# A two-layer decoder step on one core: the opening of layer 0 laid by contraction tile inside the projection, activations loaded first

## The chip, the cores and the metric

One core of a Trainium2 chip runs the whole program in one launch. The metric is device time in microseconds (us) of that core, and lower is better. The kernel before has been run three times: 2797.97, 2799.43 and 2807.59 us, median 2799.43 us.

## What is computed

Two decoder layers are applied to 1024 prompt tokens and 32 sample tokens (8 sequences of 4), 1056 in all, each 1024 wide. Only the head of layer 0 matters here:

```
mod = silu(c) @ w_ada[l] + b_ada[l]
sh1, sc1, g1, sh2, sc2, g2 = split(mod, 6)
h = rmsnorm(x, g_norm1[l]) * (1 + sc1) + sh1
p = h @ w_in[l] + b_in[l]
```

There are nine conditions: one for all prompt tokens, and one for each of the 8 samples. So sh1 and sc1 are 1024 x 9 numbers each, and every one of them is a sum over 1024 rows of w_ada. The columns of p go to three groups of heads; then follow an output projection, a second normalisation, an MLP and two residuals. The forgetting attention of the samples also needs the running sums of cached log-forget values, which are fetched by page ("past sums") for both layers at once.

## The kernel before, in words

**Layout.** Activations lie feature-major: 128 partitions, 8 contraction tiles (KT) of 1056 tokens. A full-precision product is made of three: each operand is split into a high and a low part, and high x high, high x low and low x high are added in PSUM. `part_product` (L303 to L309) issues these three matmuls for one contraction tile and one third (352) of the tokens. A panel is 128 output columns: 8 tiles x 3 thirds x 3 products = 72 matmuls. Its weights come by DMA into `raw`, GpSimd copies the high part (`split_high`, L291), VectorE subtracts it (`split_low`, L297).

**The opening (L384 to L557)** is a block of its own, which ends with all engines meeting. SyncE loads the conditions, then the first 8 blocks of w_ada (1 MB each, 256 columns each) through four buffers, with the constants and the two halves of x between them. In the order of `TURN` the four blocks of sc1 come first, then the four of sh1. For every block i, TensorE does `rows` (L469; the 9 conditions against 256 columns, 8 matmuls on column strips of the array), ScalarE copies the result (L455), TensorE does `fold` (L480; adds the four strips and turns them to columns), and VectorE adds the bias into `mod` (L532). Beside this, ScalarE squares x and VectorE adds the squares (L177, L186), TensorE sums them over partitions (L203), ScalarE takes the root (L231), VectorE the reciprocal (L546), and TensorE spreads it to all partitions (L215). Two tiles are scaled by it already here (L254). The past sums are made here too: a gather by GpSimd (L441), a scan by VectorE (L526), an offset by TensorE (L489), an addition (L538) and eight stores (L396).

**The projection (from L700)** is the next block. Its ScalarE shifts and scales each tile with `mod` (L241), then rounds it to the high part (L243); its VectorE scales the rows and makes the low part (`scale_rows`, L256; `lower_half`, L245). The 256 sample values of each partition go apart (`sample_columns`, L260). TensorE does panels 0 and 1 together in `panel_pair` (L340), tile by tile; then L1014; then panels 2 to 20 (L853), one third after another, with pieces of other work between the thirds. SyncE first stores the whole of x to `x_spill` (L741), since later panels overwrite it, and stage `out_and_mlp` loads it again.

**What sets the order.** Each engine has one queue in program order, and waits on semaphores. VectorE's list for layer 0 of the projection is: low part of panel 1's weights, the rows, the bias, `split_low(2)`, `split_low(3)`, `log_forget`, `split_low(4)`, `maxima`, `split_low(5)`, `averages(0)`, `split_low(6)`, and so on. Panel n can't start before `split_low(n)`.

Of the kernel before, what the change touches and what calls it, by code (L numbers as in the profile page):

```python
# [59 lines left out]
def trunk(nc, xT, cT, consts, suffix, params, g_final, w_first, first_params, w_ada, next_params, w_in, w_out, w_ff, state, hist, kv, lfT, pages,  # L60
# [47 lines left out]
    wada = [tile(f"wada{s}", [P, KT, 256], aL0 + 8192 * s) for s in range(4)]  # L108
# [48 lines left out]
    few = tile("few", [P, KT, NS], F0 + 20 * ROW + 2048)  # L157
    plain = [tile(f"plain{s}", [P, SEQ], F0 + (8 + s) * ROW) for s in range(4)]
# [30 lines left out]
    i_in, i_x, i_con, i_cond, i_sig, i_cs = (sem(f"start_{n}") for n in ("loaded", "rows_in", "constants", "conditions", "sigmoid", "silu"))  # L189
    i_seg, i_scan, i_off, i_sum, i_out, i_suf = (sem(f"start_{n}") for n in ("segments", "scanned", "offsets", "sums", "sums_out", "suffix"))  # L190
    i_g = [sem(f"start_gathered{l}") for l in range(LAYERS)]
    a_loaded = [sem(f"start_ada{s}") for s in range(4)]
    a_done, a_taken, a_folded, a_moved, a_padded = (sem(f"start_ada_{n}") for n in ("done", "taken", "folded", "moved", "padded"))
    pages_n = lfT.shape[0] // LAYERS
    HP = HC * PG
    Glf = [tile(f"Glf{l}", [P, HC, PG], aH0 + 4 * HP * l) for l in range(LAYERS)]
    seg = tile("seg", [P, HC, PG], aH0 + 4 * HP * LAYERS)
    suf = tile("suf", [P, P], aH0 + 4 * HP * (LAYERS + 1))
    none = tile("none", [(8 - HC) * NB, PAST // 4], aH0 + 4 * HP * (LAYERS + 1) + 512)
    first_rows = [tile(f"first_rows{s}", [P, 256], T0 + 1024 * s) for s in range(2)]  # L200
    cw = tile("cw", [P, KT, 32], T0 + 2048)
    sig = tile("sig", [P, KT * 9], T0 + 3072)
# [33 lines left out]
    def modulate(act, N, sc, sh, tiles=range(KT)):  # L236

        for k in tiles:
            t = plain[k % 4]
            act.wait_ge(N["scaled"], k + 1)  # L240
            nc.scalar.activation(t[:], t[:], ACT.Identity, scale=mod[:, sc + k, 0:1], bias=mod[:, sh + k, 0:1]).then_inc(N["modded"], 1)  # L241
            act.wait_ge(N["modded"], k + 1)
            nc.scalar.activation(aH[:, k, 0:SEQ], t[:], ACT.Copy).then_inc(N["high"], 1)  # L243

    def lower_half(dve, N, k):  # L245

        dve.wait_ge(N["high"], k + 1)
        nc.vector.tensor_tensor(aL[:, k, 0:SEQ], plain[k % 4][:], aH[:, k, 0:SEQ].bitcast(F32), ALU.subtract).then_inc(N["low"], 1)

    def scale_tile(dve, N, k):  # L250

        if k >= 4:
            dve.wait_ge(N["low"], k - 3)
        nc.vector.tensor_tensor(two(plain[k % 4][:]), two(x[:, k, 0:SEQ]), PS[:, 6:8, :], ALU.mult).then_inc(N["scaled"], 1)  # L254

    def scale_rows(dve, N, sc, sh):  # L256

        link = chain_on(dve, N["chain"])

        def sample_columns():  # L260
            f4 = few[:].rearrange("p k (b t) -> p k b t", b=NB)
            token = lambda first: mod[:, first:first + KT, 1:9].rearrange("p k (b o) -> p k b o", o=1).to_broadcast([P, KT, NB, NT])
            rs_ = PS[:, 5, 480:512].rearrange("p (o n) -> p o n", o=1).to_broadcast([P, KT, NS])
            link(nc.vector.tensor_tensor(few[:], x[:, :, SEQ:TOK], rs_, ALU.mult))
            link(nc.vector.tensor_tensor(f4, f4, token(sc), ALU.mult))
            link(nc.vector.tensor_tensor(f4, f4, token(sh), ALU.add))
            link(nc.vector.tensor_copy(aH[:, :, SEQ:TOK], few[:]))
            nc.vector.tensor_tensor(aL[:, :, SEQ:TOK], few[:], aH[:, :, SEQ:TOK].bitcast(F32), ALU.subtract).then_inc(N["few"], 1)
        scale_tile(dve, N, SCALED_EARLY)
        sample_columns()  # L270
        lower_half(dve, N, 1)
        for k in range(SCALED_EARLY + 1, KT):
            scale_tile(dve, N, k)
            lower_half(dve, N, k - 1)
        lower_half(dve, N, KT - 1)
# [64 lines left out]
    def panel_pair(pe, s, N, high, low):  # L340

        for k in range(KT):
            pe.wait_ge(N["low"], k + 1)
            if k == 0:
                for p in range(2):
                    pe.wait_ge(s["split"], p + 1)
                    for part in range(NCH - 1):
                        part_product(p, part, k, high, low)
                pe.wait_ge(N["few"], 1)
            for p in range(2):  # L350
                for part in range(NCH - 1 if k == 0 else 0, NCH):
                    last = part_product(p, part, k, high, low)
                if k == KT - 1:
                    last.then_inc(s["done"], NCH)

# [18 lines left out]
    BLOCKS = 2 * KT // 2  # L374
    first = len(sems)
    i_norm.update(norm("norm1", ROOTS + ("scaled", "modded", "high", "low")))
    SCALED_EARLY = 2
    i_par = sem("in_parameters")
    i_w, first_load, first_high, first_low = stream("in", lambda n: w_in[n:n + 1])
    TURN = [BLOCKS // 2 + i for i in range(BLOCKS // 2)] + list(range(BLOCKS // 2))  # L380
    SUMMED_AT, SPREAD_AT = 5, 6
    squared_after = {1: (0, 1, 2, 3), 2: (4, 5), 3: (6, 7)}
    OFFSETS_AT = {2: 0, 3: 1}
    with nc.Block() as block:  # L384
        @block.sync
        def _(sp):
            def ada(i):
                if i >= 4:
                    sp.wait_ge(a_done, i - 3)
                    sp.wait_ge(a_loaded[(i - 2) % 4], 16 * ((i - 2) // 4 + 1))  # L390
                sp.dma_start(wada[i % 4][:], w_first[TURN[i]]).then_inc(a_loaded[i % 4], 16)

            def sums_out(l):
# [3 lines left out]
            sp.dma_start(cs[:], cT).then_inc(i_cond, 16)  # L397
            with nc.allow_non_contiguous_dma(reason="one page a partition"):
                sp.dma_start(pcol[:], pages.rearrange("a n -> n a")).then_inc(i_cond, 16)
            ada(0)  # L400
            sp.dma_start(con[:], consts).then_inc(i_con, 16)
            sp.dma_start(nxt[:], first_params).then_inc(i_con, 16)
            ada(1)
            sp.dma_start(suf[:], suffix).then_inc(i_suf, 16)
            def rows_in(half):
                k = slice(KT // 2 * half, KT // 2 * (half + 1))
                sp.dma_start(x[:, k, :], xT[:, k, :]).then_inc(i_x, 16)
            sp.wait_ge(a_loaded[0], 16)
            rows_in(0)
            sp.wait_ge(a_loaded[1], 16)  # L410
            ada(2)
            sp.wait_ge(i_x, 16)
            rows_in(1)
            sp.wait_ge(i_seg, 3)
            for l in range(LAYERS):
                for q in range(4):
                    sp.dma_start(past_sums[l, 8 * q + HC:8 * q + 8].rearrange("r b n -> (r b) n"), none[:]).then_inc(i_out, 16)
            sp.wait_ge(a_loaded[2], 16)
            ada(3)
            sp.wait_ge(i_x, 32)  # L420
            ada(4)
            ada(5)
            first_load(sp, 0)
            ada(6)
            first_load(sp, 1)
            ada(7)
            sp.dma_start(par[:], params[0]).then_inc(i_par, 16)
            for l in range(LAYERS):
                sums_out(l)
            sp.dma_start(gfin[:], g_final).then_inc(i_in, 16)  # L430
            sp.dma_start(ptab[:], pages).then_inc(i_in, 16)
            sp.wait_ge(i_in, 32)
            sp.wait_ge(i_out, 16 * 8 * LAYERS)

        @block.gpsimd
        def _(pool):
            nc.gpsimd.memset(seg[:], 1.0).then_inc(i_seg, 1)
            nc.gpsimd.memset(none[:], 0.0).then_inc(i_seg, 1)
# [5 lines left out]
            for n in range(2):  # L444
                first_high(pool, n)

        @block.scalar
        def _(act):
            act.wait_ge(i_cond, 32)
            nc.scalar.activation(sig[:], cs[:].rearrange("p a b -> p (a b)"), ACT.Sigmoid).then_inc(i_sig, 1)  # L450
            for i in range(BLOCKS):
                act.wait_ge(a_done, i + 1)
                if i >= 2:
                    act.wait_ge(a_folded, i - 1)
                nc.scalar.activation(first_rows[i % 2][:], PS[:, i % 2, 0:256], ACT.Copy).then_inc(a_taken, 1)  # L455
                if i == SUMMED_AT:
                    root(act, i_norm)
                for j in squared_after.get(i, ()):
                    act.wait_ge(i_x, 16 if j < KT // 2 else 32)
                    square(act, i_norm, j, ss, sq_last)  # L460
# [6 lines left out]
        def _(pe):  # L467
            def rows(i):
                pe.wait_ge(a_loaded[i % 4], 16 * (i // 4) + 16)  # L469
                if i >= 2:  # L470
                    pe.wait_ge(a_taken, i - 1)
# [23 lines left out]
            for i in range(BLOCKS):  # L495
                rows(i)
                if i >= 1:
                    fold(i - 1)
# [2073 lines left out]
```

## Time and profile before

| | |
|---|---|
| runs of the kernel | 2797.97, 2799.43, 2807.59 us; median 2799.43 us |
| span of the profiled execution | 2801.3 us, from first to last instruction; no time outside it is recorded |
| TensorE matmul busy | 2711.2 us (97%) |
| VectorE, ScalarE, GpSimd busy | 1234.9, 644.0, 263.6 us |
| mean granted TensorE clock | 0.987 |
| DMA | 295.37 MB, mean 105 GB/s |

The last instruction's chain is nearly all TensorE. So the time is read by stretches: where TensorE waits, and what releases it.

### The profile page before, as it was taken

The numbers are of one execution on the slowest core, as the hardware profiler recorded it, in microseconds if no ns is written. First come the engines' busy times: TensorE is split into PE (matmuls) and PEld (weight loads), VectorE is DVE, ScalarE is ACT, GpSimd is POOL, SyncE is SP. The second block draws the span as 40 slices with busy tenths as digits, with TensorE's granted clock in tenths as the row PEclk, the third lists the DMA queues.
The fourth block names the chain that finished last, engine by engine and source line by source line (L and its number), as shares of the span: only waits on it lengthen the run. The fifth ranks groups of instructions, "written<-read, shape, count | busy, mean of one in ns | idle before, by whom it ended". The sixth has DMA issues, their size and how long they took to land. (4 is left out here: it accounts for less than half of the span.)

```text
span 2801.3 us, 48407 instructions
## 1 busy us (share of the span) xinstructions
PE 2711.2 (97%) x20524; PEld 2531.6 (90%) x20524; DVE 1234.9 (44%) x2205; ACT 644.0 (23%) x1058; POOL 263.6 (9%) x344
## 2 busy tenths in 40 slices
PE   5999989999999999999999999899999999999998
PEld 4999976699999999999989999666999999999998
DVE  5625535557423423324457354456563243242344
ACT  4334324423101101001132442343221000000012
POOL 1101100020000000001111110001100000000010
PEclk9999999999999999999999999899999999999999
DMA  8440159731222221111134101895212111111111
GB/s 310 151 108 31 67 211 328 265 115 40 82 91 85 82 91 58 56 46 46 61 112 118 51 31 62 296 347 214 75 49 79 46 46 50 42 59 46 46 55 69
DMA packets 106873, 295.37 MB, mean 105 GB/s; under 512 B 19605, under 2 KB 32790, under 8 KB 104610
## 3 DMA queue, kind: packets, MB, share of 16 engines
q1 hardware_dynamic: 106498, 291.49, 30.6%
q8 instruction: 163, 2.67, 0.4%
q0 software_dynamic: 160, 0.79, 0.1%
q14 instruction: 52, 0.43, 0.0%
HBM read 269.61 MB, written 22.63 MB: 104 GB/s over the span
## 5 line engine op out<-in xcount | busy, mean ns | idle before, releaser
L307 PE MATMUL PS<-hH,whi 128*128 128x352 f32 x1632 | 533.9, 327 | 8.2 <-DVE hL L2300 6.6
L307 PE MATMUL PS<-hL,whi 128*128 128x352 f32 x1632 | 524.9, 322 | 0.0
L307 PE MATMUL PS<-hH,wlo 128*128 128x352 f32 x1632 | 524.5, 321 | 0.0
L307 PE MATMUL PS<-aH,whi 128*128 128x352 f32 x1344 | 439.9, 327 | 4.0 <-PEq L384 3.5
L307 PE MATMUL PS<-aL,whi 128*128 128x352 f32 x1344 | 432.8, 322 | 0.0
L307 PE MATMUL PS<-aH,wlo 128*128 128x352 f32 x1344 | 432.3, 322 | 0.0
L295 POOL CAST whi<-raw 128x1024 fp32r<-128x1024 f32 x158 | 167.1, 1058 | 1660.1 <-PE PS L307 1332.7
L307 PEld LDWEIGHTS PS<-hH,whi 128*128 128x128 f32 x1632 | 307.4, 188 | 16.9 <-issue 12.7
L307 PEld LDWEIGHTS PS<-hL,whi 128*128 128x128 f32 x1632 | 308.0, 189 | 0.0
L307 PEld LDWEIGHTS PS<-hH,wlo 128*128 128x128 f32 x1632 | 307.3, 188 | 0.0
L853 PE MATMUL PS<-aH,whi 128*128 128x352 f32 x912 | 304.6, 334 | 1.9 <-ACT F L1053 1.9
L853 PE MATMUL PS<-aH,wlo 128*128 128x352 f32 x912 | 294.9, 323 | 0.0
L853 PE MATMUL PS<-aL,whi 128*128 128x352 f32 x912 | 294.6, 323 | 0.0
L307 PEld LDWEIGHTS PS<-aH,whi 128*128 128x128 f32 x1344 | 253.8, 189 | 9.4 <-issue 4.7
L307 PEld LDWEIGHTS PS<-aL,whi 128*128 128x128 f32 x1344 | 254.3, 189 | 0.0
L307 PEld LDWEIGHTS PS<-aH,wlo 128*128 128x128 f32 x1344 | 253.6, 189 | 0.0
L300 DVE TENSOR_TENSOR wlo<-raw,whi 128x1024 fp32r<-128x1024 f32 x160 | 195.6, 1223 | 130.5 <-POOL whi L295 129.0
L2384 DVE TENSOR_TENSOR aH<-ev 128x1056 fp32r<-128x1056 f32 x64 | 84.2, 1315 | 272.1 <-ACT ev L2269 272.1
L2269 ACT ACTIVATE ev<-PS 128x1056 f32<-128x1056 f32 x64 | 67.5, 1055 | 573.0 <-PE PS L307 573.0
L853 PEld LDWEIGHTS PS<-aH,whi 128*128 128x128 f32 x912 | 172.9, 190 | 8.5 <-issue 4.2
L853 PEld LDWEIGHTS PS<-aL,whi 128*128 128x128 f32 x912 | 173.3, 190 | 0.4
L853 PEld LDWEIGHTS PS<-aH,wlo 128*128 128x128 f32 x912 | 173.0, 190 | 0.0
(369 smaller groups left out, 3633.7 us busy)
## 6 DMA issues: line engine op xcount, KB each, us to landing
KVp<-kv SPq DMA_DIRECT2D x256, 384.0 KB, 7.2
raw<-w_ff SPq DMA_DIRECT2D x128, 512.0 KB, 3.6
raw<-w_in SPq DMA_DIRECT2D x42, 512.0 KB, 3.6
wad_single<-w_ada SPq DMA_DIRECT2D x40, 512.0 KB, 3.6
wad<-w_ada SPq DMA_DIRECT2D x32, 512.0 KB, 5.6
x_spill<-x SPq DMA_DIRECT2D x2, 4224.0 KB, 14.0
wada<-w_first SPq DMA_DIRECT2D x8, 1024.0 KB, 6.8
raw<-w_out SPq DMA_DIRECT2D x16, 512.0 KB, 4.4
```

The source lines that it names most:

```text
L295: nc.gpsimd.tensor_copy(home(n)[0][:], raw[spot(n)][:]).then_inc(s["high"], 1)
L300: nc.vector.tensor_tensor(wl[:], raw[spot(n)][:], wh[:].bitcast(F32), ALU.subtract).then_inc(s["split"], 1)
L307: last = nc.tensor.matmul(PS[:, 3 * p + part, 0:CW], w[:, k, :], a[:, k, part * CW:(part + 1) * CW], start=k == 0 and w is wh and a is hig ...
L853: last = nc.tensor.matmul(PS[:, part, 0:CW], w[:, k, :], a[:, k, part * CW:(part + 1) * CW], start=k == 0 and w is whi[n % 2] and a is aH, ...
L2269: nc.scalar.activation(three(ev[n % 2][:]), banks(n % 2), ACT.Relu).then_inc(s["room"], NCH)
L2384: link(nc.vector.tensor_tensor(aH[:, j, :], t, t, ALU.mult))
```

## The change

- The opening's block is gone; its work is issued at the head of the projection's block in layer 0.
- SyncE loads x first, in four quarters, then the constants, then the 8 blocks of w_ada with at most two on the way, each in a buffer of its own. The host lays w_first out so that block k holds the 128 columns of sh1 and the 128 of sc1 for contraction tile k.
- `modulate` is split differently: VectorE multiplies x by the scale and by the root in one instruction (`scale_tile`), ScalarE adds the shift and rounds (`higher_half`), VectorE adds the shift and subtracts (`lower_half`). There are 3 buffers `plain` in place of 4.
- TensorE goes through the tiles: `rows(k + 2)`, two thirds of panels 0 and 1 for tile k (12 matmuls), `fold(k + 2)`. The last thirds of both panels (48 matmuls) come after all tiles.
- The past sums move behind the opening: GpSimd gathers after `few`; VectorE scans before `split_low(3)` and adds the offsets after `split_low(4)`; TensorE makes the offsets in panel 3; the stores are issued at panel 6.
- Layer 0 no longer stores x to `x_spill`; it is loaded again from the input.

The core of the diff:

```diff
-    wada = [tile(f"wada{s}", [P, KT, 256], aL0 + 8192 * s) for s in range(4)]
+    wada = [tile(f"wada{k}", [P, KT, 256], a) for k, a in enumerate((aL0 + 4 * ROW, aL0 + 6 * ROW, aH0 + 4 * ROW, aH0 + 6 * ROW,
+                                                                     F0 + 15 * ROW, F0 + 17 * ROW, T0 + 2 * ROW, T0))]
...
+    def scale_tile(dve, N, k):
+
+        if k >= len(plain):
+            dve.wait_ge(N["low"], k - len(plain) + 1)
+        nc.vector.scalar_tensor_tensor(two(plain[k % len(plain)][:]), two(x[:, k, 0:SEQ]), mod[:, SC1 + k, 0:1], PS[:, 6:8, :], ALU.mult, ALU.mult)\
+            .then_inc(N["scaled"], 1)
+
+    def higher_half(act, N, k):
+
+        act.wait_ge(N["scaled"], k + 1)
+        nc.scalar.activation(aH[:, k, 0:SEQ], plain[k % len(plain)][:], ACT.Identity, bias=mod[:, SH1 + k, 0:1]).then_inc(N["high"], 1)
...
+        def on_sync(sp):
+            sp.dma_start(cs[:], cT).then_inc(i_cond, 16)
...
+            for q in range(4):
+                k = slice(KT // 4 * q, KT // 4 * (q + 1))
+                sp.dma_start(x[:, k, :], xT[:, k, :]).then_inc(i_x[q], 16)
+            sp.dma_start(con[:], consts).then_inc(i_con, 16)
+            sp.dma_start(nxt[:], first_params).then_inc(i_con, 16)
+            for k in range(KT):
+                if k >= BEFORE:
+                    sp.wait_ge(i_w[k % 2], 16 * (k // 2))
+                sp.dma_start(wada[k][:], w_first[k]).then_inc(i_w[k % 2], 16)
+                if k < 2:
+                    load(sp, k)
...
+        def on_pool(pool):
+            nc.gpsimd.memset(none[:], 0.0).then_inc(i_seg, 1)
+            for n in range(2):
+                split_high(pool, n)
+            pool.wait_ge(N["scaled"], KT)
+            pool.wait_ge(N["few"], 1)
             nc.gpsimd.memset(seg[:], 1.0).then_inc(i_seg, 1)
...
+        def on_tensor(pe):
...
+            def two_thirds(k):
+                pe.wait_ge(N["low"], k + 1)
+                for n in range(2):
+                    if k == 0:
+                        pe.wait_ge(s["split"], n + 1)
+                    for part in range(2):
+                        last = part_product(n, part, k, aH, aL)
+                return last
...
+            sum_squares(pe, N, ss, sq_last[(KT - 1) % 2])
+            rows(0)
+            spread_roots(pe, N)
+            fold(0)
+            rows(1)
+            fold(1)
+            for k in range(KT):
+                if k + 2 < KT:
+                    rows(k + 2)
+                last = two_thirds(k)
+                if k + 2 < KT:
+                    fold(k + 2)
+            last.then_inc(s["done"], 4)
+            pe.wait_ge(N["few"], 1)
+            for n in range(2):
                 for k in range(KT):
...
+                    last = part_product(n, NCH - 1, k, aH, aL)
+                last.then_inc(s["done"], 1)
...
+            def modulation(k):
+                dve.wait_ge(a_folded, k + 1)
...
+                nc.vector.tensor_tensor(mod[:, k:2 * KT:KT, :], folded, b, ALU.add).then_inc(a_moved, 1)
...
+                nc.vector.scalar_tensor_tensor(m, m, 1.0, g, ALU.add, ALU.mult).then_inc(a_gained, 1)
+                dve.wait_ge(a_gained, k + 1)
+            modulation(0)
+            dve.wait_ge(N["spread"], 2)
+            scale_tile(dve, N, 0)
+            split_low(dve, 0)
+            split_low(dve, 1)
+            for k in range(1, KT):
+                modulation(k)
+                scale_tile(dve, N, k)
+                lower_half(dve, N, k - 1)
+            sample_columns(dve, N)
+            lower_half(dve, N, KT - 1)
...
-                sp.dma_start(x_spill, x[:]).then_inc(spilled, 16)
+                    sp.dma_start(x_spill, x[:]).then_inc(spilled, 16)
+                else:
+                    open_sync(sp)
+                    sp.wait_ge(N["few"], 1)
...
+                if not begun:
+                    scans(dve)
                 split_low(dve, 3)
                 log_forget()
                 split_low(dve, 4)
+                if not begun:
+                    add_offsets(dve)
...
-                    sp.dma_start(x[:, :, COLS[ph]], x_spill[:, :, COLS[ph]]).then_inc(reload, 16)
+                    sp.dma_start(x[:, :, COLS[ph]], (x_spill if l else xT)[:, :, COLS[ph]]).then_inc(reload, 16)
```

## Rows read from the trace of the kernel before

**Rows 1.** Windows, panels 0 and 1; columns: stretch, PE, PEld, DVE, ACT, POOL busy, clock, DMA.

```profile
53.10:79.20 26.10, 25.66 (x144) 25.21 (x145) 18.06 (x20) 15.82 (x14) 1.77 (x2) 0.89 0.71 244
```

**Rows 2.** Waits of TensorE, 0 to 330 us; columns: waiter, releaser, sum us, times, longest.

```profile
PE PS L474 <- DMA wada<-w_first: 22.7, 4, 6.8
PE PS L307 <- PEq L384: 3.5, 1, 3.5
PE PS L853 <- ACT F L1053: 1.9, 1, 1.9
```

**Rows 3.** Windows, one stretch of the opening; the last column is GB/s.

```profile
8.00:10.00 2.00, 0.71 (x8) 0.00 (x0) 0.00 (x0) 0.38 (x1) 0.00 (x0) 1.00 1.02 410
```

**Rows 4.** Timeline of TensorE's opening and of L1014; columns: start, us, instructions.

```profile
40.05 1.02 PE L485 MATMUL PS<-con,first_rows 128*128 128x9 f32 x4
41.01 1.08 PE L207 MATMUL PS<-squares,con 128*32 128x256 f32 x8
...
42.95 1.91 PE L474 MATMUL PS<-wada,cw 128*32 128x256 f32 x16
...
45.76 0.70 PE L221 MATMUL PS<-roots,con 32*128 32x256 f32 x4 [0.16 <-DVE roots L546]
...
47.43 1.07 PE L474 MATMUL PS<-wada,cw 128*32 128x256 f32 x16
48.43 1.19 PE L485 MATMUL PS<-con,first_rows 128*128 128x9 f32 x8
...
79.22 0.81 PE L1014 MATMUL PS<-con 128*128 128x384 f32 x2
```

**Rows 5.** Groups of instructions, 0 to 53 us; busy us and mean ns, then idle.

```profile
L186 DVE TENSOR_TENSOR squares<-squares,square_last 128x1056 f32<-128x1056 f32 x6 | 7.5, 1256 | 8.5 <-ACT square_last L177 8.2
L177 ACT ACTIVATE square_last<-x 128x1056 f32<-128x1056 f32 x7 | 7.2, 1074 | 4.7 <-DMA x<-xT 4.3 <-DVE squares L186 0.4
...
L526 DVE TENSOR_TENSOR_SCAN Glf<-seg,Glf 128x768 f32<-128x768 f32 x2 | 3.4, 1746 | 7.5 <-DMA Glf<-lfT,pcol 7.5
...
L546 DVE RECIPROCAL roots<-roots 128x288 f32<-128x288 f32 x1 | 2.0, 1952 | 2.5 <-ACT roots L234 2.5
L538 DVE TENSOR_TENSOR Glf<-Glf,PS 128x768 f32<-128x768 f32 x2 | 1.9, 944 | 0.0
...
L532 DVE TENSOR_TENSOR mod<-PS,nxt 128x18 f32<-128x18 f32 x8 | 1.3, 173 | 7.5 <-PE PS L485 7.5
```

**Rows 6.** Timeline, two neighbouring matmuls of panels 0 and 1.

```profile
60.10 0.32 PE L307 MATMUL PS<-aH,whi 128*128 128x352 f32 x1
60.26 0.32 PE L307 MATMUL PS<-aL,whi 128*128 128x352 f32 x1
```

**Rows 7.** Windows around the start of panel 2; the clock is third from last.

```profile
80.00:82.00 2.00, 0.11 (x2) 0.12 (x2) 1.22 (x1) 1.85 (x2) 1.65 (x2) 1.00 0.66 243
82.00:84.00 2.00, 2.00 (x10) 2.00 (x11) 0.00 (x0) 0.00 (x0) 1.88 (x3) 0.69 0.50 160
84.00:86.00 2.00, 2.00 (x8) 2.00 (x8) 0.00 (x0) 0.99 (x1) 1.94 (x5) 0.50 0.29 117
```

**Rows 8.** Groups of VectorE by form, 1380 to 1480 us: layer 1's norm.

```profile
L633 DVE SCALAR_TENSOR_TENSOR aL<-end_wide,mod,aH 128x704 fp32r<-128x704 f32 x8 | 7.4, 944 | 0.0
L623 DVE SCALAR_TENSOR_TENSOR end_wide<-x,mod,PS 128x704 f32<-128x704 f32 x8 | 7.4, 940 | 0.0
```

**Rows 9.** Timeline of VectorE: first of the five sample instructions, and what follows them.

```profile
55.23 0.41 DVE L264 TENSOR_TENSOR few<-x,PS 128x256 f32<-128x256 f32 x1
...
57.26 1.22 DVE L248 TENSOR_TENSOR aL<-plain,aH 128x1024 fp32r<-128x1024 f32 x1
```

**Rows 10.** Timeline of VectorE and GpSimd in panels 3 to 5 of layer 0.

```profile
101.84 2.27 DVE L1193 TENSOR_TENSOR_SCAN F<-Mrow,LC 6x1024 f32<-6x1024 f32 x1
...
115.32 1.21 DVE L300 TENSOR_TENSOR wlo<-raw,whi 128x1024 fp32r<-128x1024 f32 x1
...
124.33 1.04 POOL L295 CAST whi<-raw 128x1024 fp32r<-128x1024 f32 x1 [12.60 <-PE PS L853]
```

More of the change, by code:

```diff
@@ L156, in trunk @@
     rr = tile("roots", [P, NQ + NS], F0 + 20 * ROW)
-    few = tile("few", [P, KT, NS], F0 + 20 * ROW + 2048)
-    plain = [tile(f"plain{s}", [P, SEQ], F0 + (8 + s) * ROW) for s in range(4)]
+    few = tile("few", [P, KT, NS], F0 + 21 * ROW)
+    plain = [tile(f"plain{s}", [P, SEQ], F0 + (8 + s) * ROW) for s in range(3)]
     def scale_and_gain(first, gain):
@@ L256, in scale_rows @@
-    def scale_rows(dve, N, sc, sh):
-        link = chain_on(dve, N["chain"])
[L260 to L275, printed above, removed]
+        nc.vector.scalar_tensor_tensor(aL[:, k, 0:SEQ], plain[k % len(plain)][:], mod[:, SH1 + k, 0:1], aH[:, k, 0:SEQ].bitcast(F32),
+                                       ALU.add, ALU.subtract).then_inc(N["low"], 1)
@@ L338, in panel_by_tile @@
             after(n)
[L340 to L354, printed above, removed]
     def emptied_panel(act, s, n, func):
@@ L382, in trunk, with opening, sums_out @@
[L382 to L393, printed above, removed]
+    def opening(s, N, load, split_high, split_low, par_loaded):
+        BEFORE = 2
+        def on_sync(sp):
+            sp.dma_start(cs[:], cT).then_inc(i_cond, 16)
+            with nc.allow_non_contiguous_dma(reason="one page a partition"):
+                sp.dma_start(pcol[:], pages.rearrange("a n -> n a")).then_inc(i_cond, 16)
+            for q in range(4):
[9 more added lines that the diff above has]
+                    load(sp, k)
+            sp.dma_start(par[:], params[0]).then_inc(par_loaded, 16)
+            sp.dma_start(suf[:], suffix).then_inc(i_suf, 16)
+            sp.dma_start(gfin[:], g_final).then_inc(i_in, 16)
+            sp.dma_start(ptab[:], pages).then_inc(i_in, 16)
+            sp.wait_ge(i_seg, 1)
+            for l in range(LAYERS):
+                for q in range(4):
+                    sp.dma_start(past_sums[l, 8 * q + HC:8 * q + 8].rearrange("r b n -> (r b) n"), none[:]).then_inc(i_out, 16)
+        def sums_out(sp):
+            for l in range(LAYERS):
@@ L443, in _, with on_scalar @@
                                         element_offset=l * pages_n * HP).then_inc(i_g[l], 16)
[L444 to L448, printed above, removed]
+        def on_scalar(act):
             act.wait_ge(i_cond, 32)
             nc.scalar.activation(sig[:], cs[:].rearrange("p a b -> p (a b)"), ACT.Sigmoid).then_inc(i_sig, 1)
[L451 to L460, printed above, removed]
-            act.wait_ge(a_padded, 3)
-            act.wait_ge(a_moved, BLOCKS // 2 + 1)
-            act.wait_ge(i_out, 16 * 8 * LAYERS)
-            modulate(act, i_norm, SC1, SH1, range(1))
@@ L511, in _, with take @@
-        @block.vector
-        def _(dve):
+            for j in range(KT):
+                act.wait_ge(i_x[j // 2], 16)
+                square(act, i_norm, j, ss, sq_last)
+            root(act, N)
+            def take(k):
+                act.wait_ge(a_done, k + 1)
+                if k >= 2:
+                    act.wait_ge(a_folded, k - 1)
+                nc.scalar.activation(first_rows[k % 2][:], PS[:, 2, 256 * (k % 2):256 * (k % 2) + 256], ACT.Copy).then_inc(a_taken, 1)
+            take(0)
@@ new lines, in on_scalar, with rows, fold @@
+            take(1)
+            for k in range(KT):
+                higher_half(act, N, k)
+                if k + 2 < KT:
+                    take(k + 2)
+        def on_tensor(pe):
+            def rows(k):
+                pe.wait_ge(i_w[k % 2], 16 * (k // 2 + 1))
+                if k >= 1:
+                    pe.wait_ge(a_taken, k)
+                for i in range(KT):
+                    q = i % 4
+                    last = nc.tensor.matmul(PS[32 * q:32 * q + 32, 2, 256 * (k % 2):256 * (k % 2) + 256], cw[:, i, :], wada[k][:, i, :],
+                                            start=i < 4, stop=i >= 4, skip_group_check=True)
+                last.then_inc(a_done, 1)
+            def fold(k):
+                pe.wait_ge(a_taken, k + 1)
+                if k >= 1:
+                    pe.wait_ge(a_moved, k)
+                for n in range(2):
+                    at_ = 32 * (k % 2) + 16 * n
+                    last = nc.tensor.matmul(PS[:, 5, at_:at_ + 9], first_rows[k % 2][:, n * P:(n + 1) * P], c("fold"), start=True, stop=True,
+                                            skip_group_check=True)
+                last.then_inc(a_folded, 1)
+            def two_thirds(k):
[6 more added lines that the diff above has]
+                return last
+            pe.wait_ge(a_padded, 2)
+            pe.wait_ge(i_con, 32)
+            pe.wait_ge(i_norm["added"], KT - 2)
+            pe.wait_ge(i_norm["squared"], KT)
+            sum_squares(pe, N, ss, sq_last[(KT - 1) % 2])
[4 more added lines that the diff above has]
+            fold(1)
+            for k in range(KT):
+                if k + 2 < KT:
+                    rows(k + 2)
+                last = two_thirds(k)
+                if k + 2 < KT:
+                    fold(k + 2)
+            last.then_inc(s["done"], 4)
+            pe.wait_ge(N["few"], 1)
+            for n in range(2):
+                for k in range(KT):
+                    last = part_product(n, NCH - 1, k, aH, aL)
+                last.then_inc(s["done"], 1)
@@ L513, in _, with offsets, on_vector @@
+        def offsets(pe, l):
+            if l == 0:
+                pe.wait_ge(i_suf, 16)
+            pe.wait_ge(i_scan, l + 1)
+            nc.tensor.matmul(PS[:, 4, 8 * l:8 * l + HC], suf[:], Glf[l][:, :, PG - 1], start=True, stop=True).then_inc(i_off, 1)
+        def on_vector(dve):
             nc.vector.memset(cw[:], 0.0).then_inc(a_padded, 1)
@@ L735, in projection @@
         key_of = lambda u: 1 if u == CH else 0
+        if not begun:
+            open_sync, sums_out, open_pool, open_scalar, open_tensor, offsets, open_vector, scans, add_offsets = \
+                opening(s, N, load, split_high, split_low, par_loaded)
         with nc.Block() as block:
@@ L755, in _ @@
                             load_ada(i)
+                    if n == 6 and not begun:
+                        sums_out(sp)
                     if n == 8:
@@ L797, in _ @@
                     pool.sem_inc(s["high"], 2)
+                else:
+                    open_pool(pool)
                 nc.gpsimd.memset(R3[:], 0.0).then_inc(zeroed, 1)
-                pool.wait_ge(N["scaled"], KT)
-                pool.wait_ge(N["few"], 1)
-                pool.wait_ge(spilled, 16)
+                if begun:
+                    pool.wait_ge(N["scaled"], KT)
+                    pool.wait_ge(N["few"], 1)
+                    pool.wait_ge(spilled, 16)
                 nc.gpsimd.memset(Z, 0.0).then_inc(zeroed, 1)
@@ L805, in _ @@
                 pool.wait_ge(s["high"], 3)
+                if not begun:
+                    for i in range(LAYERS):
+                        pool.wait_ge(i_g[i], 16)
                 pool.wait_ge(s["room"], NCH)
@@ L1027, in _ @@
                     conditions(3 * (n - 2) + 1)
+                    if n == 3 and not begun:
+                        for i in range(LAYERS):
+                            offsets(pe, i)
                     if 1 <= u <= CH:
@@ L1127, in _ @@
                         root_heads(CH)
+                    if n == 6 and not begun:
+                        act.wait_ge(i_out, 16 * 8 * LAYERS)
                     if n == 14:
@@ L1382, in _ @@
                 else:
[L1383 to L1384 removed]
+                    open_vector(dve)
                 dve.wait_ge(par_loaded, 16)
@@ L2527 @@
         "consts": constants(), "suffix": page_suffix(), "params": params, "g_final": a["g_final"].reshape(KT, P).T,
-        "w_first": tiles_of(a["w_ada"][0:1, :, 0:3 * DM], 256)[0], "first_params": lead[0], "w_ada": w_ada.reshape(L * 48, P, KT, P),
+        "w_first": np.concatenate([first[0::2], first[1::2]], axis=3), "first_params": lead[0], "w_ada": w_ada.reshape(L * 48, P, KT, P),
         "next_params": next_params,
```

191 lines of the change are left out of this document (45 added, 146 removed).

## The prediction, made before the changed kernel was run

> **What bounds the kernel now.** I read the waits of TensorE over the first 330 us first, then the windows around the seams, then the timeline of each engine in the opening. The waits [rows 2] show where layer 0 loses time: 22.7 us until w_ada blocks land, 3.5 us at the meeting of the engines at the end of the opening's block, and 1.9 us before panel 2. The view's other three waits sum to 1.7 us and lie in the opening too: once panel 2 runs, TensorE waits for nobody up to 330 us and sets the pace. From 53.10 to 79.20 it does panels 0 and 1 (144 matmuls, 25.66 of 26.10 us busy) [rows 1], then L1014, and panel 2 begins at 79.22 + 0.81 + 1.9 = 81.9 [rows 2, 4]. So the whole question is one number: **when does panel 2 begin?** Before: 81.9. All else of the 2801.3 us span should shift with it. The sum is made against that span; the median of the runs is 2799.4, so I take 1.9 off at the end, as a shift of the profiled execution.
>
> There is a second loss at that seam. While TensorE sits idle before panel 2 the clock is still granted at 1.00; then it falls, with a mean of 0.69 from 82 to 84 and 0.50 from 84 to 86 [rows 7]. At 0.50 matmuls run at 1.2 instead of 2.4 GHz: 0.6 + 1.0 us are lost, about 1.7 with the rest behind 86. A changed kernel that comes to panel 2 without a gap saves them. Its mark is therefore 81.9 + 1.7 = **83.6**: later than that is a slower kernel.
>
> **The change, part by part.** *Loads.* The DMA engines move about 410 GB/s in the opening [rows 3]. Conditions and x are 4.36 MB; with a start at 3.3 us and 0.6 us to signal (both estimates), the last quarter is there at 3.3 + 10.6 + 0.6 = 14.5. Constants come at 16.5, block 0 at 19.1, block 1 and panel 1's weights by 24.5, and one more block each 2.6 us: block 7 at about 40. Two on the way are enough for that rate if a block's issue costs under 2.6 us beyond the one before; else it is at most double, 5.2 us, still no more than what comes below.
>
> *Head.* Two squares after the last quarter (2 x 1.07) with the last addition (1.26) beside and behind them [rows 5]: 17.2. The sums take 41.01 to 42.95 [rows 4]: 19.1. Root 0.5, reciprocal 1.95 [rows 5]: 21.7; `rows(0)` lies beside it. The spread goes from 45.76 to 47.4 [rows 4]: 23.3. `fold(0)` is behind it in TensorE's queue: 1.0 at the slow rate [rows 4]: 24.3. Then VectorE: `modulation(0)` is two small instructions of 0.17 to 0.2 [rows 5], each waited for, 0.46: 24.8; `scale_tile(0)`.
>
> Its cost, and that of the new `lower_half`, is bounded by 0.94 for 704 columns [rows 8] and by that per column for 1024, 1.37; the old instruction on 1024 took 1.22 [rows 9]. I take 1.24, near the one of equal size. So 26.0; two `split_low` (2 x 1.2): 28.4; `modulation(1)`, `scale_tile(1)`, `lower_half(0)`: **31.3**, when the first 12 matmuls start. Before, they started at 53.1, so here 22 us seem won.
>
> *The turn.* They are mostly given back, because the loop closes on itself. VectorE's list is modulation(k), scale(k), low(k-1). Modulation(k) needs fold(k). Fold(k) stands in TensorE's queue behind the 12 matmuls of tile k-2. These wait for low(k-2), which VectorE issued just before modulation(k). No two of these steps of one turn can lie beside each other: 12 matmuls, fold, modulation, scale, low. The matmuls are 0.16 apart at full clock [rows 6], so 1.9, and 3.8 at half; a fold is 0.6 (half of 1.19) or 1.0 [rows 4]. Full clock: 1.9 + 0.6 + 0.46 + 1.24 + 1.24 = **5.4 us**. Half clock: 3.8 + 1.0 + 2.94 = **7.7 us**. Only `rows` (1.07 or 1.91 [rows 4]) and ScalarE's work lie in the shade of VectorE's. Six turns lead from low(0) to low(6): 33 us or 46 us.
>
> *Which clock?* In a turn at full clock TensorE does 1.9 + 0.6 + 1.07 = 3.6 us of 5.4 and is idle for nearly 2 us: as long as the idle time after which the clock fell before [rows 2, 7]. At half clock it is busy for 6.7 of 7.7 us, which should bring the clock back, as it came back in panels 0 and 1, whose mean was 0.89 [rows 1]. So I expect it to go up and down, with about half of the turns slow: 6.6 us a turn. Low(6) is then at 31.3 + 39.6 = 70.9.
>
> *Tail.* The sample columns now stand before low(7): 57.26 - 55.23 = 2.0 [rows 9], and low(7) 1.2: 74.1. Then 12 matmuls, 2.8 between the clocks: 76.9; the last thirds, 48 x 0.16 = 7.7, plus 0.9 for a clock that is still low at first: 85.5; L1014, 0.8: **86.3**. The 1.9 us wait before panel 2 goes, for panel 0's `done` now comes 24 matmuls (3.8 us) before the end and the high and low parts of panel 2's weights (about 2.3 us) fit in. That needs `raw` of panel 2 in time: it is issued after `few`, 13 us before the end, behind two short loads; GpSimd has two memsets, two gathers and two more memsets before it, about 5.4 us. Both are covered by about 3 us. If this cover is gone, the load of panel 2's weights is next late and costs what it is late by; the wait of 1.9 us above is the size of it.
>
> *Behind the opening.* No spill of 4.3 MB: nobody on TensorE's path waits for it, 0 us. Past sums: scans 3.4 us [rows 5] while VectorE waits for panel 3's weights: 0. Additions 2 x 0.94 [rows 5], but VectorE first waits for offsets which TensorE makes only after the second third of panel 3, some 10 us into that panel; `maxima`, which began at 101.84, begins about 7 us later in its panel. Behind it stands `split_low(5)`: 115.32 + 1.2 = 116.5 before, now like 123.5, and panel 5 started at about 124.3 (GpSimd's release by panel 4) [rows 10]. It fits by 0.8 us. I take 0; between 0 and 3 us if a step there is longer. The stores' wait in ScalarE (panel 6) has over 15 us of room: 0.
>
> *Sum.* 86.3 against the mark of 83.6: +2.7; the profiled execution would span 2804.0. 2799.4 + 2.7 = **2802 us**. No change that can be told: a measurement here tells about 0.5%, 14 us.
>
> **Rivals.**
> (a) *The clock stays up through the loop.* For it: TensorE is busy for two thirds of each turn. Then 31.3 + 33 + 3.2 + 1.9 + 7.7 + 0.8 = 77.9, that is -5.7: **2794**. Chance 0.25.
> The Trainium skill (TensorE: Matmul & The Clock Gate, HAM oscillation) describes a loop over contraction tiles whose clock falls in every tile, because the wait between bursts is long; by its rule waits as short as this loop's should leave the clock up, which is this rival. The drop after 1.9 us of idle time [rows 2, 7] speaks against it.
> (b) *The clock stays at half to the end of the opening* (slower side). Place: the turns and last thirds. 31.3 + 46 + 3.2 + 3.8 + 15.4 + 0.8 = 100.5, +17: **2816** (2809 if the last thirds recover). Against it: panels 0 and 1 came back by themselves. It decides from the point at which more than four in five of these matmuls are slow. Chance 0.12.
> (c) *The loop doesn't close*, because I misread an order, and the loads set the pace: block 7 at 40, then 1.1 + 0.6 + 0.5 + 1.2 + 1.2 + 2.0 + 1.2 + 1.9 + 7.7 + 0.8 = 58; TensorE's own work from 31.3 (144 matmuls, 6 rows, 6 folds, 33 us) sets 65: -18, **2781**. For it: each engine alone has less than 3.7 us a turn. Chance 0.07.
> (d) *Past sums stall a panel*: the 0.8 us of cover is gone, at `split_low(5)` or a raw load behind it, +3 to +8: **2807**. Chance 0.09.
> (e) *My case*, the closed loop with a clock that goes up and down: 0.47.
>
> **How the numbers follow.** The likeliest is 2802. From (a), less 4 us for its terms, to (b) the range is 2790 to 2813, which leaves out (c) and the far end of (b). My case alone holds 2796 to 2808. Faster by over 0.5% is (c) alone with a little of (a): 0.08. Slower by over 0.5% is half of (b) and a tail of (d): 0.07. The rest, 0.85, is within 0.5%.
>
> **What would show it.** In the changed profile: first matmuls of L307 at about 31; groups of 12 that start 5.4 to 7.7 us apart, each released by VectorE's aL; modulation's L532-like instruction released by TensorE's fold; a granted clock between 0.5 and 1.0 from 31 to 77; panel 2 at 82 to 90 without a wait; nothing waiting from panel 3 to 8; all after that in step with before. Groups less than 4.5 us apart would refute the closed loop; a wait at L853 for wlo would show (d).

## The result and the profile after

The changed kernel takes 2810.25 us (median of 16 runs, 2803.23 to 2816.47); the kernel before, run beside it, takes 2800.98 us (16 runs). The ratio is 1.0031, 95% interval 1.0022 to 1.0040: 9.3 us slower. The forecast was 2802 us, in 2790 to 2813. The profiled execution spans 2807.8 us against 2801.3, so it shows 6.5 of the 9.3 us. One of the 7 runs of e_both (10470.59 us) and one of the 12 of e_no_spill (14026.16 us) were slow; they stand in no ratio, and move the medians given below by less than 0.1 us.

The waits of TensorE over the first 330 us of the changed kernel (against [rows 2]; columns: waiter, releaser, sum us, times, longest):

```profile
PE PS L209 <- DVE squares L187: 17.6, 1, 17.6
PE PS L298 <- DVE aL L253: 14.3, 7, 3.0
PE PS L968 <- DMA wad<-w_ada: 2.5, 3, 1.9
PE PS L223 <- DVE roots L487: 0.9, 1, 0.9
PE PS L435 <- ACT first_rows L410: 0.5, 1, 0.5
```

The waits for w_ada blocks in the opening, the 3.5 us at the block's end and the 1.9 us before panel 2 are gone. In their place stand 17.6 us until the squares are summed, seven waits for the low part of a tile, and one that [rows 2] don't have: 2.5 us for w_ada blocks at L968, which is in the panels behind the opening.

**The turn of the loop.** Timeline of the changed kernel, one turn (start, us, engine; L298 is the 12 matmuls, L435 fold, L425 rows, L494 and L498 modulation, L242 scale, L253 low part, L248 ScalarE):

```profile
43.89 1.07 PE L425 MATMUL PS<-wada,cw 128*32 128x256 f32 x16
44.00 0.18 DVE L494 TENSOR_TENSOR mod<-PS,nxt 128x18 f32<-128x18 f32 x1 [3.99 <-PE PS L435]
44.21 0.17 DVE L498 SCALAR_TENSOR_TENSOR mod<-mod,nxt 128x9 f32<-128x9 f32 x1
44.42 1.28 DVE L242 SCALAR_TENSOR_TENSOR plain<-x,mod,PS 128x1024 f32<-128x1024 f32 x1
45.61 1.28 DVE L253 SCALAR_TENSOR_TENSOR aL<-plain,mod,aH 128x1024 fp32r<-128x1024 f32 x1
45.73 1.15 ACT L248 ACTIVATE aH<-plain,mod 128x1024 fp32r<-128x1024 f32 x1 [0.32 <-DVE plain L242]
46.95 0.43 PE L298 MATMUL PS<-aH,whi 128*128 128x352 f32 x1 [1.98 <-DVE aL L253]
...
48.96 0.51 PE L435 MATMUL PS<-con,first_rows 128*128 128x9 f32 x4
49.51 0.18 DVE L494 TENSOR_TENSOR mod<-PS,nxt 128x18 f32<-128x18 f32 x1 [2.62 <-PE PS L435]
```

VectorE's modulation begins when fold ends, the matmuls begin when its low part ends (1.98 us idle), fold follows the matmuls, and the next modulation begins 5.51 us after this one. Each step starts where the one before it ends. The groups of 12 start at 33.1, 40.1, 47.0, 52.5, 59.3, 64.8 and 70.3: three turns of 5.5 us, in which the 12 matmuls stand 0.16 us apart behind the first, and three of 6.8 to 6.9, in which some stand 0.29 us apart; 6.2 in the mean. The first long turn begins at that slow rate, though the clock column still reads 1.00 there (the matmuls start at 33.59, 33.88, 34.18); behind it the clock falls at about 40, 53 and 70 us (windows; the clock is third from last; compare [rows 7]):

```profile
40.00:42.00 2.00, 1.93 (x7) 0.50 0.80 239
52.00:54.00 2.00, 1.54 (x8) 0.83 0.04 8
54.00:56.00 2.00, 2.00 (x10) 0.50 0.00 0
70.00:72.00 2.00, 1.71 (x6) 0.60 0.00 0
140.00:142.00 2.00, 0.26 (x12) 1.00 0.83 336
142.00:144.00 2.00, 1.56 (x32) 0.52 0.35 57
146.00:148.00 2.00, 2.00 (x9) 0.50 0.83 295
148.00:150.00 2.00, 2.00 (x12) 0.77 0.45 176
```

Panel 2 begins without a wait and at full clock (timeline of TensorE):

```profile
83.43 0.81 PE L1000 MATMUL PS<-con 128*128 128x384 f32 x2
84.30 0.43 PE L839 MATMUL PS<-aH,whi 128*128 128x352 f32 x1
```

84.3 stands against the mark of 83.6: the opening itself costs +0.7 us in this execution. The traces bear the mark out: the fold after the first third of panel 3 starts at 101.29, before at 100.45, 0.8 us later.

**Behind the opening.** Nearly all of the rest is lost between 139 and 149 us. TensorE's timeline there, and SyncE's queue:

```profile
139.07 0.73 PE L975 MATMUL PS<-con,mid_rows 128*128 128x9 f32 x6
141.74 0.78 PE L968 MATMUL PS<-wad,cs 128*9 128x128 f32 x16 [1.94 <-DMA wad<-w_ada]
142.89 1.04 PE L968 MATMUL PS<-wad,cs 128*9 128x128 f32 x16 [0.37 <-DMA wad<-w_ada]
144.15 1.04 PE L968 MATMUL PS<-wad,cs 128*9 128x128 f32 x16 [0.22 <-DMA wad<-w_ada]
145.12 0.66 PE L839 MATMUL PS<-aH,whi 128*128 128x352 f32 x1
```

```profile
134.89 0.33 SPq L280 DMA_DIRECT2D raw<-w_in  x1
135.27 10.32 SPq L723 DMA_DIRECT2D wad<-w_ada  x6
```

Before, the same places of SyncE's queue read:

```profile
126.66 0.33 SPq L289 DMA_DIRECT2D raw<-w_in  x1
129.30 11.11 SPq L748 DMA_DIRECT2D wad<-w_ada  x6
```

The load at 134.89 is load(7); it waits for `split_low(6)`. It is 8 us later than before, and the three w_ada blocks that TensorE takes at the end of panel 5 are issued behind it. Before, they were issued 9.1 us before their use at 138.4, now 4.5 us before TensorE is ready for them at 139.8. TensorE waits 1.94 + 0.37 + 0.22 = 2.5 us. Then the clock is low from about 142 to 149: at half clock over 6.8 us, 3.4 us are lost. How far behind the kernel before TensorE is afterwards can be read from the next blocks of w_ada (first line before, second after):

```profile
153.23 1.50 PE L982 MATMUL PS<-wad,cs 128*9 128x128 f32 x48
160.20 1.50 PE L968 MATMUL PS<-wad,cs 128*9 128x128 f32 x48
```

That is 7.0 us: 0.8 from the opening, 0.5 since the four matmuls of the offsets (0.61 us at 107.31) now stand in panel 3 (the next fold is at 115.50 against 114.21, 1.3 us late), and 5.7 from the wait and the slow clock behind it. The spans differ by 6.5: later stages give 0.5 us back, no more than they vary from one execution to the next (e_sums_early below).

Why `split_low(6)` is late shows in VectorE's timeline of the changed kernel:

```profile
103.55 1.23 DVE L291 TENSOR_TENSOR wlo<-raw,whi 128x1024 fp32r<-128x1024 f32 x1
107.96 1.82 DVE L525 TENSOR_TENSOR Glf<-Glf,PS 128x768 f32<-128x768 f32 x2 [3.19 <-PE PS L474]
109.70 2.27 DVE L1184 TENSOR_TENSOR_SCAN F<-Mrow,LC 6x1024 f32<-6x1024 f32 x1
```

It stands 3.19 us for the offsets, then adds for 1.8. `maxima` begins at 109.70, before at 101.84 [rows 10]; `split_low(6)` begins at 133.63, before at 125.41.

### The profile page after: what moved, and what is told of

Same layout as the page of the kernel before. It is cut to its first block and busy times, and to the rows that moved or that the text cites. A ratio compares the mean times of both kernels' runs of the same rounds, so it can differ in the third digit from the quotient of the medians.

```text
span 2807.8 us, 48394 instructions
## 1 busy us (share of the span) xinstructions
PE 2710.1 (97%) x20524; PEld 2531.2 (90%) x20524; DVE 1240.9 (44%) x2212; ACT 635.5 (23%) x1050; POOL 265.8 (9%) x344
## 5 line engine op out<-in xcount | busy, mean ns | idle before, releaser
L298 PE MATMUL PS<-hH,whi 128*128 128x352 f32 x1632 | 534.0, 327 | 7.5 <-DVE hL L2294 6.0
L298 PE MATMUL PS<-hL,whi 128*128 128x352 f32 x1632 | 525.1, 322 | 0.0
L298 PE MATMUL PS<-hH,wlo 128*128 128x352 f32 x1632 | 524.7, 322 | 0.0
L298 PE MATMUL PS<-aH,whi 128*128 128x352 f32 x1344 | 441.2, 328 | 14.4 <-DVE aL L253 14.3
L298 PE MATMUL PS<-aL,whi 128*128 128x352 f32 x1344 | 433.6, 323 | 0.0
L298 PE MATMUL PS<-aH,wlo 128*128 128x352 f32 x1344 | 433.2, 322 | 0.0
L298 PEld LDWEIGHTS PS<-hH,whi 128*128 128x128 f32 x1632 | 307.6, 188 | 16.0 <-issue 12.2
L298 PEld LDWEIGHTS PS<-hL,whi 128*128 128x128 f32 x1632 | 308.2, 189 | 0.0
L298 PEld LDWEIGHTS PS<-hH,wlo 128*128 128x128 f32 x1632 | 307.5, 188 | 0.0
L298 PEld LDWEIGHTS PS<-aH,whi 128*128 128x128 f32 x1344 | 254.6, 189 | 22.7 <-DVE aL L253 17.7
L298 PEld LDWEIGHTS PS<-aL,whi 128*128 128x128 f32 x1344 | 255.0, 190 | 0.0
L298 PEld LDWEIGHTS PS<-aH,wlo 128*128 128x128 f32 x1344 | 254.2, 189 | 0.0
```

Source lines behind the costliest of these rows:

```text
L298: last = nc.tensor.matmul(PS[:, 3 * p + part, 0:CW], w[:, k, :], a[:, k, part * CW:(part + 1) * CW], start=k == 0 and w is wh and a is hig ...
```

## The experiments

All runs of the kernel before that stand beside these lie at a median of 2800.4 us (first four experiments) and 2801.25 us (last four).

**e_sums_early.**

```diff
                     third(n, 0)
+                    if n == 2 and not begun:
+                        pe.wait_ge(s["room"], 2 * NCH)
+                        for i in range(LAYERS):
+                            offsets(pe, i)
...
-                    if n == 3 and not begun:
-                        for i in range(LAYERS):
-                            offsets(pe, i)
...
                 split_low(dve, 3)
+                if not begun:
+                    add_offsets(dve)
                 log_forget()
                 split_low(dve, 4)
-                if not begun:
-                    add_offsets(dve)
```

> The changed kernel with the offsets made on TensorE after the first third of panel 2 and added on VectorE right behind split_low(3), where VectorE was idle for 2.2 us before it could begin log_forget. The opening is untouched. Theory (queue): the offsets held up VectorE by 5 us, so split_low(6) was late, SyncE stood at load(7) behind it, and the w_ada blocks that panel 5 needs were issued late: TensorE waited 2.5 us and then ran 6.8 us at half clock (3.4 us lost). It expects no wait for w_ada in layer 0, no fall of the clock at about 142 us, and 5 to 6 us less than the changed kernel, so within 0 to +4 us of the kernel before. Rival (the slower opening alone makes the difference): no more than 1 us less than the changed kernel.

Measured: 2803.34 us (11 runs), ratio to before 1.0010 (1.0001 to 1.0019): 6.9 us less than the changed kernel, +3.0 against before. No wait for w_ada in the first 330 us, and the clock stays up (windows; clock third from last):

```profile
140.00:142.00 2.00, 2.00 (x53) 1.00 0.28 47
142.00:144.00 2.00, 2.00 (x14) 1.00 0.99 365
```

The additions have gone into VectorE's idle time before `log_forget`, which shrinks from 2.2 to 0.46 us (its timeline):

```profile
91.97 1.81 DVE L525 TENSOR_TENSOR Glf<-Glf,PS 128x768 f32<-128x768 f32 x2
94.24 0.71 DVE L1169 TENSOR_SCALAR lf<-F 128x1056 f32<-128x1056 f32 x1 [0.46 <-ACT logs L1111]
```

The profiled execution spans 2801.1 us, as before, with panel 2 at 84.3. At 154.56 us it does the w_ada blocks shown above for 153.23, 1.3 us late; it makes that up only in later stages, with a mean granted clock of 0.988 against 0.987. So where the past sums stand costs some 6 us, and what is left of the change about 3 by the medians (0 to 5 by the interval).

**e_queue.**

```diff
-            loads_at = {2: (0,), 5: (1,), 6: (2, 3), 7: (4, 5), 8: (6,), 9: (7,)}
+            loads_at = {2: (0,), 5: (1,), 6: (2, 3), 7: (5,), 8: (6,), 9: (7,)}
...
                         sums_out(sp)
+                        for i in groups[4][1]:
+                            load_ada(i)
```

> The changed kernel with one thing moved on SyncE's queue: the three w_ada blocks of group 4 are issued before load(7) instead of behind it. VectorE's delay by the offsets stays. Theory (queue): the wait for w_ada and the half clock behind it go as in e_sums_early, 5 to 6 us less than the changed kernel. Rival (VectorE's delay itself holds TensorE up through split_low): the wait moves to a wlo of panel 5 to 7 and the time stays.

Measured: 2804.45 us (11 runs), ratio 1.0013 (1.0004 to 1.0022), 5.8 us less than the changed kernel. SyncE's queue:

```profile
134.12 1.28 SPq L723 DMA_DIRECT2D wad<-w_ada  x3
138.42 0.33 SPq L280 DMA_DIRECT2D raw<-w_in  x1
```

VectorE is as late as in the changed kernel; load(7) is issued 3.5 us later still (138.42), as panel 2 is here. No wait for w_ada is left, and none appears at any wlo: the way from VectorE's delay to TensorE led through SyncE's queue alone.

This profile shows one more thing. Its opening is the changed kernel's, word for word, but panel 2 begins at 87.8, not 84.3. Its groups of 12 start at 32.9, 40.2, 47.3, 54.3, 61.2, 68.1 and 73.6: five long turns and not three. The clock fell in more of them (windows):

```profile
40.00:42.00 2.00, 1.78 (x6) 0.58 0.64 180
56.00:58.00 2.00, 2.00 (x12) 0.65 0.00 0
```

So the opening costs +0.7 us in one execution and +4.2 in another. The +3.0 us of e_sums_early's median lies between the two; its profile caught an execution with the smaller cost.

**e_fold_first.**

```diff
                 if k + 2 < KT:
                     rows(k + 2)
-                last = two_thirds(k)
-                if k + 2 < KT:
                     fold(k + 2)
+                last = two_thirds(k)
```

> The changed kernel with fold(k + 2) ahead of the 12 matmuls of tile k in TensorE's queue, so that the modulation of tile k + 2 no longer stands behind them. Theory (closed loop): the turn falls from a mean of 6.2 us to what the longest single engine needs, TensorE's 1.9 + 1.1 + 0.5 = 3.5 us at full clock, and the clock stays up since TensorE is hardly idle; seven turns give 16 to 19 us back. The w_ada blocks come 3.4 us apart and would not bind. Rival (the loads or VectorE's own work set the turn): a turn of 5 us or more and less than 8 us gained. The wait for w_ada in panel 5 should be there as before.

Measured: 2796.33 us (11 runs), ratio 0.9985 (0.9976 to 0.9994): 13.9 us less than the changed kernel, the only part of this study so far that beats the kernel before. Panel 2 begins at 70.9, 13.4 us earlier. A turn is 4.1 us, not 3.5 (TensorE's timeline):

```profile
45.29 0.61 PE L435 MATMUL PS<-con,first_rows 128*128 128x9 f32 x4 [0.50 <-ACT first_rows L410]
...
49.41 0.61 PE L435 MATMUL PS<-con,first_rows 128*128 128x9 f32 x4 [0.50 <-ACT first_rows L410]
```

Fold now waits 0.50 us for ScalarE's copy of the rows just made: seven times, where the changed kernel has one such wait. The expectation left it out, and the gain was 13.9 us and not 16 to 19. The wait for w_ada (2.8 us here) stays, as expected.

**e_fill.** It adds eight matmuls that open a group of their own in the bank where panel 0's first third is being summed. The expectation holds that nothing reads their columns, but this kernel's sums are not those of the others, so it tells of the time alone.

```diff
+                for f in range(8 if 1 <= k < KT - 1 else 0):
+                    nc.tensor.matmul(PS[:, 0, CW:512], whi[0][:, 0, :], aH[:, 0, 0:512 - CW], start=True, stop=True, skip_group_check=True)
                 last = two_thirds(k)
```

> The changed kernel with eight matmuls without use (160 columns, into columns of a bank that nothing reads) on TensorE before the 12 matmuls of tiles 1 to 6, where it is idle for 2 us. Their order against the others is unchanged. Theory (clock): the clock no longer falls in the loop and each turn takes 5.4 to 5.6 us instead of 5.5 or 6.9; 3 to 4 us less than the changed kernel, if the eight take less than the idle time. Rival (the long turns have another cause): the turns stay mixed. If the eight take longer than 2 us, turns grow by what is over.

Measured: 2804.96 us (11 runs), ratio 1.0017 (1.0008 to 1.0026), 5.3 us less than the changed kernel. The eight take 1.12 us and fit in (TensorE's timeline):

```profile
38.85 0.43 PE L298 MATMUL PS<-aH,whi 128*128 128x352 f32 x1 [0.93 <-DVE aL L253]
...
42.30 1.12 PE L461 MATMUL PS<-aH,whi 128*128 128x160 f32 x8
44.35 0.43 PE L298 MATMUL PS<-aH,whi 128*128 128x352 f32 x1 [0.93 <-DVE aL L253]
```

From 38.85 on the groups start 5.5 us apart each time (38.85, 44.35, 49.86, 55.37, 60.88, 66.42), and up to 65 us the clock stays full. It falls once, at tile 6, which has no `rows` beside the eight and leaves TensorE idle for 2.03 us again (timeline, then window):

```profile
66.42 0.66 PE L298 MATMUL PS<-aH,whi 128*128 128x352 f32 x1 [2.03 <-DVE aL L253]
66.00:68.00 2.00, 1.58 (x5) 0.50 0.00 0
```

Panel 2 begins at 80.2, 4.1 us before that of the changed kernel: 2.5 of them from the six turns, 1.3 from the head, where the spread of the roots met a full clock here. More work for TensorE made the program faster: the long turns of the changed kernel were a matter of the clock.

**e_both** (the two diffs together).

> e_fold_first and e_sums_early together: the loop opened and the offsets made in panel 2. Theory (two independent losses): the closed loop costs 13 to 14 us and the late w_ada blocks 5 to 6, so the two gains add: 19 to 20 us less than the changed kernel, 2790 us where the kernel before is at 2800.5, with panel 2 at 71 us and no wait for w_ada. Rival (the gains overlap, for instance since the w_ada wait only takes the place of another): 2794 to 2796.

Measured: 2790.16 us (7 runs), ratio 0.9963 (0.9950 to 0.9976): 20.1 us less than the changed kernel. 13.9 + 6.9 = 20.8 are what the two give alone. Panel 2 begins at 71.9, and no wait for w_ada appears. The losses are separate.

**e_ahead.**

```diff
             fold(1)
+            rows(2)
             for k in range(KT):
-                if k + 2 < KT:
-                    rows(k + 2)
+                if k + 3 < KT:
+                    rows(k + 3)
+                if k + 2 < KT:
                     fold(k + 2)
...
+            take(2)
             for k in range(KT):
                 higher_half(act, N, k)
-                if k + 2 < KT:
-                    take(k + 2)
+                if k + 3 < KT:
+                    take(k + 3)
```

> e_both with rows one tile further ahead of fold in TensorE's queue, so that fold(k + 2) finds its copy by ScalarE done. In e_fold_first TensorE waited seven times for 0.5 us for that copy. Theory (TensorE's own work and this wait set the turn of 4.1 us): turns of 3.6 us, 2 to 3 us less than e_both. Rival (the blocks of w_ada, which land about 3.4 us apart, or VectorE set the turn once the wait is gone): less than 1 us.

Measured: 2787.32 us (5 runs), ratio 0.9955 (0.9940 to 0.9969), 2.8 us less than e_both by the medians, though the intervals overlap. The profile shows it: no wait before fold in the turns, and turns of 3.57 us (TensorE's timeline):

```profile
39.87 1.07 PE L426 MATMUL PS<-wada,cw 128*32 128x256 f32 x16
40.87 0.61 PE L436 MATMUL PS<-con,first_rows 128*128 128x9 f32 x4
...
43.44 1.07 PE L426 MATMUL PS<-wada,cw 128*32 128x256 f32 x16
```

Panel 2 begins at 68.1. TensorE's own work now sets the turn while it makes rows and folds; only the last three tiles, which have no rows, wait for VectorE (0.61, 0.62 and 1.05 us).

**e_best.**

```diff
-            sample_columns(dve, N)
             lower_half(dve, N, KT - 1)
+            sample_columns(dve, N)
```

> e_ahead with the sample columns behind lower_half(7) on VectorE, so that the 12 matmuls of tile 7 no longer wait for them; TensorE needs them only for the last thirds. Theory: 2.0 us of VectorE's work move beside those matmuls: 1 to 2 us less than e_ahead, and about 2786 in all. Rival: few comes later, and with it SyncE's load of panel 2's weights and GpSimd's chain before split_high(2); then a wait appears before panel 2 and nothing is gained.

Measured: 2787.78 us (5 runs), ratio 0.9952 (0.9937 to 0.9967): the same as e_ahead. Panel 2 begins at 65.3, 2.8 us earlier than in e_ahead, but the span is 2786.0 against 2784.4. New waits of 0.3 and 0.6 us for w_ada appear around 98 and 99 us: the panels have moved ahead of the loads. At 137.00 us it is still 1.36 us ahead of e_ahead (the same w_ada blocks, there at 138.36). The rest goes in a later stage, where the clock falls here and stays at 1.00 in e_ahead (windows of e_best):

```profile
316.00:320.00 4.00, 3.24 (x16) 0.75 0.01 2
352.00:356.00 4.00, 4.00 (x17) 0.57 0.00 0
```

No run here tells whether the edit brings on these falls or the one execution did; the interval of the medians is wider than the gain that was looked for.

**e_no_spill.**

```diff
-                sp.dma_start(x_spill, x[:]).then_inc(spilled, 16)
+                if begun:
+                    sp.dma_start(x_spill, x[:]).then_inc(spilled, 16)
...
-                    sp.dma_start(x[:, :, COLS[ph]], x_spill[:, :, COLS[ph]]).then_inc(reload, 16)
+                    sp.dma_start(x[:, :, COLS[ph]], (x_spill if l else xT)[:, :, COLS[ph]]).then_inc(reload, 16)
```

> The kernel before with only this of the change: layer 0 doesn't store x to x_spill and loads it again from the input. All theories of the working expect the same time within 1 us, since nobody on TensorE's path waits for the store. A gain of 2 us or more would mean that the store of 4.3 MB slowed something in panels 0 and 1, and that this part of the change helps.

Measured: 2800.3 us (12 runs), ratio 0.9993 (0.9983 to 1.0004): no difference. The 4.3 MB store was hidden.

## Why the prediction was right or wrong

**The one number.** Panel 2 was forecast for 86.3 and came at 84.3 (87.8 in the profile of e_queue, with the same opening). The reason given, a loop that closes on itself under a clock that goes up and down, is what the traces show. The closeness is in part luck: the head came 1.8 us later than forecast, the six turns took 2.4 less, and the tail 1.4 less.

**The time.** 2810.25 us lies inside 2790 to 2813, but outside the 2796 to 2808 that my case alone was said to hold. The range reached so far up for rival (b), a clock at half to the end of the opening, which didn't happen; that it holds the result is luck. And "no change that can be told" was wrong: with 16 runs of each kernel the interval of the ratio (1.0022 to 1.0040) leaves out 1.

**Head.** The squares were ready at 17.6 (forecast 17.2); the first 12 matmuls started at 33.1, not 31.3. Most of that is the spread of the roots: 2.8 us, from 22.3 to 25.1, not 1.6. The 1.6 us of [rows 4] came from a stretch at full clock (`rows` takes 1.07 there), while the fold behind it was put at the slow rate. In e_fold_first and e_fill, where the clock is up at 22 us, the spread takes 1.6, and the matmuls start at 31.6 and 31.8. The two new VectorE instructions take 1.28 us on 1024 columns, but start 1.19 apart, so the forecast's 1.24 cost nothing; the 0.5 us that the second fold waited held up nobody.

**The turn.** Forecast 5.4 us at full clock, measured 5.5. The 7.7 at half clock was too high: where it fell, a turn took 6.8 to 6.9, since not all of a turn was slow: the 12 matmuls took 3.5, 3.4 and 3.0 us, not 3.8, and only one of the three folds was slow (0.86 us against 0.51). Half of the turns were long, as forecast, but the mean was 6.2, not 6.6. That these five steps can't lie beside each other is shown by e_fold_first: one line moved, 13.9 us.

**The clock.** It went up and down, as in my case. Rival (a), a clock that stays up, failed: TensorE idled 2.0 us in a turn (3.0 in the last) and the clock fell in some. The page TensorE: Matmul & The Clock Gate of the Trainium skill (HAM oscillation), by which gaps as short as these leave the clock alone, doesn't fit these rows. Rival (b) failed as well: it came back each time. e_fill gives the price: 5.3 us by the medians, where 3 to 4 were expected; in its profile 2.5 us come from the turns and 1.3 from the head.

**Tail and seam.** The wait before panel 2 went, and the slow matmuls behind it too, as forecast. Taking the mark at 83.6 and not at 81.9 was needed: 84.3 against 81.9 would read as 2.4 us lost, where the folds of panel 3 show 0.8.

**Spill.** Forecast 0; measured 0 (e_no_spill).

**Past sums: here the working failed.** The step is "It fits by 0.8 us. I take 0", with 0 to 3 us as bounds. VectorE's wait for the offsets and the fit of `split_low(5)` were right: `maxima` came 7.9 us later, 5.5 of them in its panel (forecast 7), and `split_low(5)` ended at 125.3, panel 5 began at 125.9. What I did not follow was the next queue: SyncE's load(7) waits for `split_low(6)`, and w_ada blocks stand behind it. I had compared each `split_low` with the panel that reads it, but not with the load that waits for it. Measured: 2.5 us of wait and 3.4 us of slow clock behind it in the profile; 6.9 us (e_sums_early) and 5.8 us (e_queue) by the medians. The 0.5 us that the offsets' own matmuls cost TensorE in panel 3 are missing from the sum too. Rival (d) had the price, +3 to +8, and the delay behind a raw load, but it got 0.09 and named the wrong thing that is late: "a wait at L853 for wlo" never came; the wait was for w_ada.

So the sum should have read +3 for the opening, as it did (+2.7), and +6 for the sums, which it put at 0: 9 us, as measured. "Nothing waiting from panel 3 to 8" was wrong.

## What to carry to other kernels

Before a pipelined loop is interleaved across engines, write one turn as a ring: for each step, what its own queue puts ahead of it and what that waits for. If the ring passes from engine to engine, the turn is the sum of its steps and not the work of the busiest engine; here it was 5.5 us against 3.6, and moving one small step ahead of the long one in its queue opened it (4.1 us a turn, and 3.6 with the rows made one tile earlier). When work is moved into an engine's idle time, follow its delay through the queues of those who wait for it, the DMA issuing queue first, and count a short wait of TensorE together with the slow matmuls behind it.

## What the runs showed of the hardware

The granted clock of TensorE fell to half in a loop whose idle times were only 2.0 us (3.0 before the last fall), and it fell in other turns from one execution to the next (panel 2 at 84.3 and at 87.8 with the same opening). With 1.12 us of matmuls without use in each idle time, which left 0.93 us idle, it stayed up through five of them in one profile (e_fill), and fell after the sixth, where 2.03 us were left. And a wait of 2.5 us in three pieces at 140 us was followed by 6.8 us at half clock: the clock (3.4 us) cost more than the wait.
